# Another order of filler blocks, mLSTM chunks and two waits in the mixer of a transformer layer

## The reference

```
z = rms_norm(x) @ w_in      # z_qa, z_kv, z_kpe, zq, zk, zv, zi, zf, zo, gate_a, gate_b
y_a = mla_attention(rms_norm(z_qa) @ w_qb, rms_norm(z_kv) @ w_kvb, rope(z_kpe))   # 16 heads, 8 pairs
qk  = silu(causal_dwconv(concat(zq, zk)))                                         # 4 taps
y_b = rms_norm(mlstm(qk, zv, zi, zf)) * sigmoid(zo)                               # 8 heads, 4 passes of 2
x   = x + (sigmoid(gate_a) * (y_a @ p_a) + sigmoid(gate_b) * (y_b @ p_b)) @ w_out
x   = x + cross_attention(x, mem);   x = x + conv_glu_ffn(x)
```

## Time and profile before

| | us |
|---|---|
| median of 3 runs | 1897.83 |
| lowest and highest run | 1894.16, 1900.44 |
| span of the profiled execution | 1896.2 |
| TensorE busy | 1827.0 |
| VectorE busy | 1086.0 |
| ScalarE busy | 950.1 |

### The profile page before, as it was taken

One profiled execution on the slowest core, in us unless ns is written; L12 is line 12 of the kernel. 1 busy time (PEld: TensorE's weight loads), 2 busy tenths in 40 slices (PEclk: granted clock), 3 DMA queues, 4 the chain that ended last, 5 costly groups with the idle time before them and its releaser, 6 DMA issues.

```text
span 1896.2 us, 30789 instructions
## 1 busy us (share of the span) xinstructions
PE 1827.0 (96%) x10920; PEld 1617.8 (85%) x10920; DVE 1086.0 (57%) x1442; ACT 950.1 (50%) x1265; POOL 4.6 (0%) x12
## 2 busy tenths in 40 slices
PE   6899999999999999999999979999999999999998
PEld 5798988888777888888788769999999999888887
DVE  5567676564664545454556855655555555555554
ACT  6656556665664444444545455444444444444442
POOL 0000000000000000000000000000000000000000
PEclk9899999999999999999999989999999999999999
DMA  5434444445445555555654434555555555455554
GB/s 204 153 133 153 151 144 149 149 144 168 132 144 168 190 196 188 189 190 197 246 200 143 136 120 162 183 181 184 178 177 177 181 186 184 168 197 190 194 193 144
DMA packets 88990, 325.48 MB, mean 172 GB/s; under 512 B 9920, under 2 KB 9920, under 8 KB 88176
## 3 DMA queue, kind: packets, MB, share of 16 engines
q1 hardware_dynamic: 88128, 319.85, 50.5%
q0 software_dynamic: 816, 4.98, 0.8%
HBM read 322.63 MB, written 2.10 MB: 171 GB/s over the span
## 4 chain that ended last, share of the span: by engine, by line
PE 88%; DVE 5%; ACT 3%; issue 2%; DMA 1%; DVEq 0%; ACTq 0%; POOL 0%; SPq 0%
PE ps L268 12%; PE ps L269 12%; PE ps L270 12%; PE ps L260 11%; PE ps L261 11%; PE ps L262 11%; PE ps L630 4%; PE ps L632 4%; PE ps L631 4%; DVE w_lo L1045 2%; DMA x_tok<-in_x 1%; PE ps L417 1%; PE ps L416 1%; ACT w_hi L653 1%; PE ps L291 1%
## 5 line engine op out<-in xcount | busy, mean ns | idle before, releaser
L1045 DVE TENSOR_TENSOR w_lo<-w_raw,w_hi 128x1024 fp32r<-128x1024 f32 x598 | 725.8, 1224 | 682.6 <-ACT w_hi L653 672.8
L653 ACT ACTIVATE w_hi<-w_raw 128x1024 fp32r<-128x1024 f32 x598 | 628.9, 1058 | 789.0 <-PE ps L262 327.8
L268 PE MATMUL ps<-u,w_hi 128*128 128x256 f32 x1744 | 499.4, 286 | 2.5 <-DVE u L1066 2.5
L270 PE MATMUL ps<-u,w_lo 128*128 128x256 f32 x1744 | 494.9, 284 | 0.0
L269 PE MATMUL ps<-u,w_hi 128*128 128x256 f32 x1744 | 494.9, 284 | 0.0
L268 PEld LDWEIGHTS ps<-u,w_hi 128*128 128x128 f32 x1744 | 336.4, 193 | 4.4 <-DVE u L1066 2.8
L269 PEld LDWEIGHTS ps<-u,w_hi 128*128 128x128 f32 x1744 | 336.5, 193 | 1.3 <-issue 1.2
L270 PEld LDWEIGHTS ps<-u,w_lo 128*128 128x128 f32 x1744 | 336.1, 193 | 0.0
L260 PE MATMUL ps<-w_hi,u 128*128 128x512 f32 x576 | 230.2, 400 | 0.8 <-ACT v_aug L822 0.8
L261 PE MATMUL ps<-w_lo,u 128*128 128x512 f32 x576 | 225.1, 391 | 0.0
L262 PE MATMUL ps<-w_hi,u 128*128 128x512 f32 x576 | 224.9, 390 | 0.0
(11 more groups left out here) (320 smaller groups left out, 2126.6 us busy)
## 6 DMA issues: line engine op xcount, KB each, us to landing
w_raw<-in_stream SPq DMA_DIRECT2D x602, 512.0 KB, 3.3
x_tok<-in_x SPq DMA_DIRECT2D x2, 1024.0 KB, 6.5
mem_tok<-in_mem POOLq DMA_DIRECT2D x2, 1024.0 KB, 7.6
x_tok<-in_x POOLq DMA_DIRECT2D x2, 1024.0 KB, 7.2
out<-x_tok SPq DMA_DIRECT2D x8, 256.0 KB, 3.6
mats<-in_mats POOLq DMA_DIRECT2D x1, 320.0 KB, 8.0
cols<-in_cols POOLq DMA_DIRECT2D x1, 257.0 KB, 7.0
gq<-in_positions POOLq DMA_DIRECT2D x1, 128.0 KB, 9.7
```

Source lines behind the costliest of these rows:

```text
L268: pe.matmul(o, w_hi[:, s, lo:hi], a_hi, start=first, stop=False, skip_group_check=True)
L270: return pe.matmul(o, w_lo[:, s, lo:hi], a_hi, start=False, stop=last, skip_group_check=True)
L653: act.activation(w_hi[:, s, :], w_raw[:, s, :], ACT.Copy).then_inc(hi_made, 1)
L1045: TTo(w_lo[:, s, :], w_raw[:, s, :], w_hi[:, s, :].bitcast(F32), ALU.subtract).then_inc(lo_made, 1)
```

## The change

The stream has the same chunks in another order.

1. The first filler block (the first half of zq) is no longer in pass 0 of attention. It stands as a block of its own (G_QK) between z_kv and attention. The transposes of the z_kv latent come behind its fifth chunk, and its convolution (`conv_first(0)`, `conv_taps(0)`) comes ahead of the memset that raises the first ya_lo.
2. The fillers move up by one pass: "qk" in passes 0 to 2, "v" in passes 3 to 6, and the first quarter of zo in pass 7 ("zo", by tokens, into bank 2). The zo block of its own goes, with its wait for v_aug (zv_read).
3. In an mLSTM pass TensorE's chunks are placed 1, 3, 4 (ahead of the scores, ahead of the products with v, ahead of the transposes) and not 2, 3, 3. The splits of ACT and DVE move accordingly.
4. TensorE waits for y_b ahead of the y_b chunks of each merge, not ahead of the first merge.
5. DVE waits for x ahead of its first additions to x, not ahead of the splits of W_out.

```diff
@@ -44,10 +44,10 @@
 G_KV = G_QA + KPB
-G_MLA = G_KV + KPB
+G_QK = G_KV + KPB
+G_MLA = G_QK + KPB
 MLA_PER = 2 + 2 + KPB
-G_ZO = G_MLA + PAIRS * MLA_PER
-G_ML = G_ZO + KPB
+G_ML = G_MLA + PAIRS * MLA_PER
 G_MERGE = G_ML + NBLK * KPB
@@ -347,7 +350,10 @@
                     mm.then_inc(sem("gates_T"), 1)
-            latent_T(1)
+            for c in range(KPB):
+                by_features(pos, G_QK + c, u, 2 * c, GEMM)
+                if c == 4:
+                    latent_T(1)
             pe.wait_ge(sem("lat_lo"), 2 * LC)
@@ -356,7 +362,7 @@
                     else:
-                        by_tokens(pos, 4 + i, u, 2 * i, KC - 1, GEMM)
+                        by_tokens(pos, 4 + i, u, 2 * i, KC - 1, GEMM if filler == "v" else GEMM + 2)
@@ -437,22 +443,17 @@
-            with pe.Fori(0, 4) as j:
+            with pe.Fori(0, 3) as j:
                 mla_pass(Pos(G_MLA, j, MLA_PER), j, "qk")
             with pe.Fori(0, 4) as j:
-                mla_pass(Pos(G_MLA + 4 * MLA_PER, j, MLA_PER), j + 4, "v")
-            pe.wait_ge(sem("zv_read"), TT * 4)
-            for c in range(KPB):
-                by_tokens(Pos(G_ZO), c, u, 2 * c, KC - 1, GEMM + 2)
+                mla_pass(Pos(G_MLA + 3 * MLA_PER, j, MLA_PER), j + 3, "v")
+            mla_pass(Pos(G_MLA + 7 * MLA_PER), 7, "zo")
...
                 by_tokens(pos, 0, u, 0, KC - 1, bank)
-                by_tokens(pos, 1, u, 2, KC - 1, bank)
@@ -465,7 +466,7 @@
                                stop=True).then_inc(sem("ml_scored"), 1)
-                for c in (2, 3, 4):
+                for c in (1, 2, 3):
                     by_tokens(pos, c, u, 2 * c, KC - 1, bank)
@@ -474,7 +475,7 @@
                 mm.then_inc(sem("ml_num"), 1)
-                for c in (5, 6, 7):
+                for c in (4, 5, 6, 7):
                     by_tokens(pos, c, u, 2 * c, KC - 1, bank)
@@ -496,6 +497,7 @@
                     by_tokens(pos, KPB + c, u, 2 * c, KC - 1, GEMM + 2)
+                pe.wait_ge(sem("yb_lo"), 4 * NBLK)
                 for c in range(KPB):
@@ -519,7 +521,6 @@
-            pe.wait_ge(sem("yb_lo"), 4 * NBLK)
             with pe.Fori(0, NBLK - 1) as j:
@@ -749,7 +750,18 @@
             latent(1, GEMM + 2)
-            latent_hi(1, kv_t, "g_kva")
+            for c in range(KPB):
+                split(pos, G_QK + c)
+                if c == 4:
+                    latent_hi(1, kv_t, "g_kva")
+            def conv_first(i):
+                for m in range(4):
+                    act.activation(qk[:, bass.ds(4 * i + m, 1) if not isinstance(i, int) else slice(4 * i + m, 4 * i + m + 1), :],
+                                   ps[:, GEMM + m // 2, (m % 2) * T:(m % 2 + 1) * T], ACT.Copy,
+                                   scale=dcol("conv_qk", 16 * i + (4 * m + 3))).then_inc(sem("cv_first"), 1)
+            conv_first(0)
@@ -807,38 +819,32 @@
                     act.wait_ge(sem("cv_taps"), 48)
-                    silu = qk[:, bass.ds(4 * (it - 4), 4), :]
+                    silu = qk[:, bass.ds(4 * (it - 3), 4), :]
                     act.activation(silu, silu, ACT.Silu).then_inc(sem("cv_made"), 1)
...
                 if filler == "qk":
-                    for m in range(4):
-                        act.activation(qk[:, bass.ds(4 * it + m, 1), :],
-                                       ps[:, GEMM + m // 2, (m % 2) * T:(m % 2 + 1) * T], ACT.Copy,
-                                       scale=dcol("conv_qk", 16 * it + (4 * m + 3))).then_inc(sem("cv_first"), 1)
-                else:
+                    conv_first(it + 1)
+                if filler == "v":
                     for t in range(TT):
-                        act.activation(v_aug[:, t, bass.ds(2 * (it - 4), 2), 0:ML_DV],
+                        act.activation(v_aug[:, t, bass.ds(2 * (it - 3), 2), 0:ML_DV],
                                        ps[:, GEMM + t, :].rearrange("p (h d) -> p h d", h=2), ACT.Copy
...
-            with act.Fori(0, 4) as j:
+            with act.Fori(0, 3) as j:
                 mla_pass(Pos(G_MLA, j, MLA_PER), j, "qk")
             with act.Fori(0, 4) as j:
-                mla_pass(Pos(G_MLA + 4 * MLA_PER, j, MLA_PER), j + 4, "v")
+                mla_pass(Pos(G_MLA + 3 * MLA_PER, j, MLA_PER), j + 3, "v")
+            mla_pass(Pos(G_MLA + 7 * MLA_PER), 7, "zo")
...
-            for c in range(KPB):
-                split(Pos(G_ZO), c)
             act.wait_ge(sem("attended"), PAIRS)
@@ -848,12 +854,13 @@
                 sigmoid_block(bank)
-                for c in range(3):
+                for c in range(2):
                     split(pos, c)
...
                     act.activation(w_ml[:, i, :], w_ml[:, i, :], ACT.Exp).then_inc(sem("ml_w"), 1)
+                split(pos, 2)
                 split(pos, 3)
@@ -864,9 +871,9 @@
                                        ).then_inc(sem("ml_ss"), 1)
-                split(pos, 5)
                 act.wait_ge(sem("ml_mv"), j + 1)
                 act.activation(tiny[:, 48:52], tiny[:, 48:52], ACT.Sqrt).then_inc(sem("ml_rt"), 1)
+                split(pos, 5)
                 split(pos, 6)
@@ -1182,7 +1189,26 @@
             latent(1)
-            latent_lo(1, kv_t, "g_kva")
+            for c in range(KPB):
+                split(pos, G_QK + c)
+                if c == 4:
+                    latent_lo(1, kv_t, "g_kva")
+            def conv_taps(i):
+                dve.wait_ge(sem("cv_first"), 4 * i + 4)
+                for tap in (2, 1, 0):
+                    lag = 3 - tap
+                    if tap < 2:
+                        dve.wait_ge(sem("cv_taps"), 12 * i + 4 * (2 - tap))
+                    for m in range(4):
+                        row = 4 * i + m
+                        dst = (qk[:, row, lag:T] if isinstance(i, int) else
+                               qk[:, bass.ds(row, 1), lag:T].rearrange("p o t -> p (o t)"))
+                        STT(dst, ps[:, GEMM + m // 2, (m % 2) * T:(m % 2 + 1) * T - lag],
+                            dcol("conv_qk", 16 * i + (4 * m + tap)), dst, ALU.mult, ALU.add
+                            ).then_inc(sem("cv_taps"), 1)
+            conv_taps(0)
             dve.memset(v_aug[:, :, :, ML_DV:DV1], 1.0).then_inc(sem("ya_lo"), 1)
@@ -1257,27 +1283,16 @@
                 if filler == "qk":
-                    dve.wait_ge(sem("cv_first"), 4 * it + 4)
-                    for tap in (2, 1, 0):
-                        lag = 3 - tap
-                        if tap < 2:
-                            dve.wait_ge(sem("cv_taps"), 12 * it + 4 * (2 - tap))
-                        for m in range(4):
-                            dst = qk[:, bass.ds(4 * it + m, 1), lag:T].rearrange("p o t -> p (o t)")
-                            STT(dst, ps[:, GEMM + m // 2, (m % 2) * T:(m % 2 + 1) * T - lag],
-                                dcol("conv_qk", 16 * it + (4 * m + tap)), dst, ALU.mult, ALU.add
-                                ).then_inc(sem("cv_taps"), 1)
-            with dve.Fori(0, 4) as j:
+                    conv_taps(it + 1)
+            with dve.Fori(0, 3) as j:
                 mla_pass(Pos(G_MLA, j, MLA_PER), j, "qk")
             with dve.Fori(0, 4) as j:
-                mla_pass(Pos(G_MLA + 4 * MLA_PER, j, MLA_PER), j + 4, "v")
-            for c in range(KPB):
-                split(Pos(G_ZO), c)
+                mla_pass(Pos(G_MLA + 3 * MLA_PER, j, MLA_PER), j + 3, "v")
+            mla_pass(Pos(G_MLA + 7 * MLA_PER), 7, "zo")
@@ -1286,7 +1301,6 @@
                 split(pos, 0)
-                split(pos, 1)
                 dve.wait_ge(sem("ml_scored"), j + 1)
@@ -1294,7 +1308,7 @@
                        a_tok[:, 1, bass.ds(2 * j + i, 1)], 0.0, ALU.add, ALU.min).then_inc(sem("ml_arg"), 1)
-                split(pos, 2)
+                split(pos, 1)
                 for i in range(2):
@@ -1303,8 +1317,8 @@
                         ).then_inc(sem("ml_p"), 1)
+                split(pos, 2)
                 split(pos, 3)
-                split(pos, 4)
                 dve.wait_ge(sem("ml_num"), j + 1)
@@ -1324,7 +1338,7 @@
                            ).then_inc(sem("ml_hn"), 1)
-                split(pos, 5)
+                split(pos, 4)
                 dve.wait_ge(sem("ml_ss"), 4 * j + 4)
@@ -1394,12 +1409,12 @@
                 for t in range(TT):
+                    if it == 0:
+                        dve.wait_ge(sem(f"x_again{t}"), 16)
                     xs = (x_tok[:, t, it * BLK:(it + 1) * BLK] if isinstance(it, int)
...
-            dve.wait_ge(sem("x_again0"), 16)
-            dve.wait_ge(sem("x_again1"), 16)
             wout_block(Pos(G_WOUT), 0, GEMM + 2)
@@ -1556,7 +1571,8 @@
     wkv = np.asarray(i["w_kvb"])[0].reshape(LORA, PAIRS, 2, 2, P)
-    fill = [q0, q0 + BLK, k0, k0 + BLK] + [v0 + n * BLK for n in range(4)]
+    fill = [q0 + BLK, k0, k0 + BLK] + [v0 + n * BLK for n in range(4)] + [o0]
+    block(w_in, q0)
     for pair in range(PAIRS):
@@ -1564,7 +1580,7 @@
         block(w_in, fill[pair])
-    for n in range(4):
+    for n in range(1, 4):
```

(31 more changed lines are left out.)

## The result

The changed kernel takes 1881.1 us (median of 4 runs, 1880.0 to 1882.1) where the one before takes 1897.3 in the same session: a ratio of 0.9915, 95% interval 0.990 to 0.993. Forecast were 1880 us and a range of 1873 to 1887. The span fell from 1896.2 to 1880.2, by 16.0 us, where the sum said 17.6.

The account below looks back on a forecast made before the run. TensorE, busy 96% of the span, was taken as the bound, through its waits and half clock. Removed 26.4 less added 8.85 gave net 17.6 us off 1896.2: 1878.6, plus 1.6 for the median, said as 1880; range 1873 to 1887.

Parts of the forecast that it names:

- the sign of being wrong: At the mLSTM scores: new stalls of over 2 us there would have shown the prediction wrong.
- cover of the latent, with half clock: Between second latent and attention: 7.7 us of TensorE wait and 2.5 us lost to half clock go, 10.2 us removed.
- wait for the memset: Third chunk of attention pass 0: TensorE waits for the v_aug memset behind the convolution taps, 3.75 us added.
- half clock behind it: Attention pass 0, behind the memset wait: one stretch of half clock, 1.6 us added, bounded by 0 and 2.6.
- one gq wait: Attention passes behind blocks of taps: four gq waits become three, 0.9 us removed.
- first wait for k_st: Entry from attention to mLSTM: ScalarE's chain to k_st outlasts the one chunk covering it, 0.85 us added.
- waits at the transposes: mLSTM passes: four TensorE waits until hn is scaled go, 5.75 us removed.
- three waits at the scores: mLSTM pass boundaries: TensorE waits for m_st or k_st, 2.65 us added over three boundaries.
- y_b, with half clock: Start of the merge: the y_b wait and the half clock after it go, 3.1 + 2.65 = 5.75 us removed.
- Step 1: Block of q columns between second latent and attention: 10.2 us removed, 3.75 added by the memset wait, 1.6 by half clock.
- Steps 3 and 4: Entry to mLSTM: 0.95 us removed, 0.85 added; mLSTM passes: 5.75 removed at transposes, 2.65 added at scores.
- step 6: Splits of W_out: TensorE's wait through DVE's wait for x goes, 2.85 us removed; chunks' lead of some 8 us gives cover.
- The rival of half clock at the new stalls: mLSTM scores: each of four new stalls draws half clock, 6.4 us more, 1886.6 us; chance 0.17.

Follow-up runs that it names:

- the second trace: The changed kernel as it is, with no edit, timed and profiled once more: 1881.7 us, ratio 0.9919 to the kernel before.

## Why the prediction was right

The time, the sign and the rows that would show it came out; the waits after are the ones that were named, with three for gq, one for the memset, four at the scores. Those four are longer than said, 0.97 to 1.44 us in the view where 0.7 to 0.8 stood, but under the 2 us that would have been the sign of being wrong. By its own terms, in us of the span:

| term | said | found | shown by |
|---|---|---|---|
| cover of the latent, with half clock | -10.2 | -10.2 | removed in the trace; 11.0 when undone |
| wait for the memset | +3.75 | +3.7 | 105.40 to 109.20 less one start; gone with its move |
| half clock behind it | +1.6 | +1.5 | 110.0 to 113.4; 6.8 us in the second trace |
| one gq wait | -0.9 | -0.9 | three of 0.76 |
| wait for v_aug in mLSTM | -0.95 | -0.95 | gone |
| first wait for k_st | +0.85 | +1.6 | 1.44 + 0.16 |
| waits at the transposes | -5.75 | -5.75 | gone; back when undone |
| three waits at the scores | +2.65 | +3.5 | 1.13, 1.28, 1.13 |
| y_b, with half clock | -5.75 | -5.9 | gone in the trace; 4.5 when undone |
| x | -2.85 | -1.85 | 2.85 removed, w_lo 1.0 longer |
| other half clock | 0 | -0.7 | two stretches fewer in attention and one new, one 3.4 us longer at 987 |

The sum of what was found is 15.95, against 16.0 in the span. The last row of it is the softest: 1.5 us a stretch in attention, and 0.8 for the longer one, worked out from the busy time of its 23 matmuls. Step 1 is right as a mechanism and in size. Steps 3 and 4 are right as mechanisms; their new waits were sized 1.6 us too short together, since the hand-over to TensorE at each score (0.15 us, or 0.25 at the entry) was left out, m_st came 0.1 us later than its chain was summed to, and at the entry VectorE was taken as idle while it was in a split and ScalarE's start behind y_a as faster than it is. As a result part 3 of the change, booked at 2.25 us, is worth 0.8 by the waits and nothing by the clock. In step 6 the term that failed is the cover of "the lead of some 8 us that a chunk has over its split": one chunk took 9.5 us beside the 2 MB of x (issued at 905.93, used at 915.49), in both traces of the changed kernel, so 1.0 us of the 2.85 came back. Runs with other edits ahead of that place had 0 to 1.0 us there, so the code of that place doesn't fix the size; that it hangs on when the transfers meet is the likely reading, and no run sets it on purpose.

That the time came within 1.1 us of the forecast is in part luck. The misses of steps 3, 4 and 6 come to 2.6 us. Of these 0.7 were made up for by half clock in places that the change doesn't touch, and 0.7 more because the median of the runs lies 0.9 us above the span of the trace, where 1.6 was taken. The one stretch that was booked behind the memset was a choice between bounds of 0 and 2.6 us: it cost 1.5 us in the first trace and 2.7 in the second.

The rival of half clock at the new stalls did not come: no stretch of it stands at a score of mLSTM in any of the seven traces that have these stalls. Nor is the drain behind a table load in the trace that the Trainium skill ("ScalarE: Activation LUTs", What ACT_TABLE_LOAD costs) describes: the rows at 447.45 and 448.74 leave it 0.01 us. What the prediction held open, whether the stall of pass 0 draws half clock, is settled: it did in all eight traces that have the stall, for 3.4 or 6.8 us.

## What to carry over

Work that depends on nothing is worth what it covers: the same block of q columns covered 11 us around the latent's chain and none of them behind it. When a chunk is moved from one gap to another, write down for each engine what then lies between the last release and the next wait, splits and hand-overs included, since the stall may only change its place: here 5.9 us of waits became 5.1, and a move of one split on two engines did what the move of a chunk had not. A semaphore that gates TensorE should be raised ahead of work that nobody waits for yet; one memset behind twelve taps cost some 5 us.

## What the runs showed of the hardware

Half clock behind a wait isn't fixed by the length of the wait. The 2.7 us at W_out drew none in the kernel before, and the wait of 3.0 us drew 3.4 us of it when it was put back; the 3.5 us of pass 0 drew 3.4 us in one trace of the changed kernel and 6.8 in another. The waits of 1.0 to 1.5 us in mLSTM drew none in any trace (in the kernel before, the last of them has the wait for y_b right behind it, and half clock there).

Half clock also comes with no wait at all. In attention it fell over the filler chunk right behind the scores. In the changed kernel the short matmuls of the scores, which follow one another without a wait, ran from 425.83 to 430.64, and the clock was at half from 430.9 to 434.3. The same scores stand in all eight passes, yet it fell in other passes in the second trace of the same kernel (179.3 and 350.0), and in none in others. One stretch costs about 1.5 us, so by the number of such stretches alone, 0 to 2, two executions of one kernel can differ by some 3 us (an estimate). A step worth less than that is to be read from its waits, not from the span.

A transfer of 512 KB that takes 3.3 us from issue to landing in the median of the whole span took 9.5 us while 2 MB came in by another queue, and 7.4 us beside the same 2 MB in two kernels whose edits lie far ahead of it.
